# Hybrid decoder layer on one core: attention values with the value matrix as stationary operand, four score banks and a deeper order of steps

## What is computed

```python
proj = jnp.einsum('bsd,de->bse', x, w_in[l])
aq, ak, av, hq, hf, hi_, hg = [proj[..., offsets[j]:offsets[j + 1]] for j in range(len(IN_SIZES))]
a = moba_attention(to_heads(aq), to_heads(ak), to_heads(av), t5_bias)   # softmax(q k / 8 + bias), causal
...
r = hgrn2(...)                                # gated recurrence, RMS norm per head, gate
mix = jnp.einsum('bse,ed->bsd', jnp.concatenate([a, r], axis=-1), w_o[l])
x = layer_norm(DEEPNORM_ALPHA * x + mix, ln1_g[l], ln1_b[l])
moe = hier_moe(x, ...)                        # top-1 group, top-2 of its experts
x = layer_norm(DEEPNORM_ALPHA * x + moe, ln2_g[l], ln2_b[l])
```

## Time and profile before

| | us |
|---|---|
| median of 3 runs (lowest, highest) | 656.98 (656.62, 657.64) |
| the profiled execution, its own time | 655.68 |
| its span | 653.9 |
| PE busy | 616.9 (94%) |
| DVE busy | 475.7 (73%) |
| ACT busy | 377.7 (58%) |
| POOL busy | 110.2 (17%) |
| attention, first scores to first matmul of the output product | 213.4 to 264.4 |

### The profile page before, as it was taken

How to read it: one execution, slowest core, us unless ns; L and a number is a source line. 1 busy time by engine, 2 the same in 40 slices (tenths; PEclk the granted TensorE clock), 3 DMA queues, 4 the chain that set the end, 5 groups by cost and what they waited for, 6 DMA issues and landing times.

```text
span 653.9 us, 9793 instructions
## 1 busy us (share of the span) xinstructions
PE 616.9 (94%) x3747; PEld 497.8 (76%) x3747; DVE 475.7 (73%) x555; ACT 377.7 (58%) x401; POOL 110.2 (17%) x78
## 2 busy tenths in 40 slices
PE   8998999999999999999799997999999999999990
PEld 7877788877767778888577886888888888888860
DVE  3758398884456434446688985889888898888867
ACT  4567333341124666321537785877787777877744
POOL 0012222480000000000077431110111111110000
PEclk9998999999999999999989998999999999999995
DMA  8732123224106000785679999999999999999353
GB/s 329 257 130 76 56 77 117 65 72 71 65 1 191 4 2 1 311 333 193 225 262 419 420 381 364 399 379 391 391 390 392 391 392 402 402 404 364 88 161 128
DMA packets 42413, 155.25 MB, mean 237 GB/s; under 512 B 11923, under 2 KB 12131, under 8 KB 30092
## 3 DMA queue, kind: packets, MB, share of 16 engines
q1 hardware_dynamic: 37500, 138.40, 54.5%
q0 software_dynamic: 4880, 16.39, 9.5%
HBM read 139.96 MB, written 14.81 MB: 237 GB/s over the span
## 4 chain that ended last, share of the span: by engine, by line
PE 78%; DMA 6%; DVE 4%; POOL 4%; ACT 4%; issue 3%; DVEq 0%; SPq 0%; POOLq 0%; ACTq 0%
PE psum L620 21%; PE psum L622 20%; PE psum L621 20%; PE psum L853 3%; PE psum L733 2%; PE psum L1003 2%; DMA misc<-x_dram,slots 2%; DMA acc_dram<-misc,slots 2%; DMA slot_dram<-rec_i,addr_i 1%; PE psum L831 1%; PE psum L763 1%; PE psum L844 1%; PE psum L1020 1%; PE psum L629 1%; POOL slot_dram L553 1%
## 5 line engine op out<-in xcount | busy, mean ns | idle before, releaser
L1669 DVE TENSOR_TENSOR w_lo<-ring,w_hi 128x2048 fp32r<-128x2048 f32 x95 | 216.1, 2289 | 24.0 <-ACT w_hi L1287 23.3
L620 PE MATMUL psum<-w_hi,act_hi 128*128 128x512 f32 x544 | 221.3, 407 | 4.5 <-ACT ring L1199 1.9
L622 PE MATMUL psum<-w_hi,act_lo 128*128 128x512 f32 x544 | 213.2, 392 | 0.0
L621 PE MATMUL psum<-w_lo,act_hi 128*128 128x512 f32 x544 | 213.1, 392 | 0.0
L1287 ACT ACTIVATE w_hi<-ring 128x2048 fp32r<-128x2048 f32 x96 | 182.4, 1916 | 25.2 <-PE psum L622 24.7
L620 PEld LDWEIGHTS psum<-w_hi,act_hi 128*128 128x128 f32 x544 | 102.9, 189 | 32.0 <-issue 4.5
L622 PEld LDWEIGHTS psum<-w_hi,act_lo 128*128 128x128 f32 x544 | 102.5, 189 | 22.2
L621 PEld LDWEIGHTS psum<-w_lo,act_hi 128*128 128x128 f32 x544 | 102.8, 189 | 18.8
L1430 DVE TENSOR_TENSOR w_lo<-ring,w_hi 128x2048 fp32r<-128x2048 f32 x17 | 41.8, 2461 | 33.5 <-ACT w_hi L1136 33.4
L579 POOL DMA_INDIRECT acc_dram<-misc,slots x15 | 24.8, 1654 | 204.2 <-ACT misc L1337 195.4
L1136 ACT ACTIVATE w_hi<-ring 128x2048 fp32r<-128x2048 f32 x17 | 32.5, 1914 | 42.4 <-PE psum L622 40.8
(11 more groups left out here) (235 smaller groups left out, 711.3 us busy)
## 6 DMA issues: line engine op xcount, KB each, us to landing
ring<-in_w_gate SPq DMA_DIRECT2D x32, 1024.0 KB, 11.6
ring<-in_w_up SPq DMA_DIRECT2D x32, 1024.0 KB, 13.5
ring<-in_w_down SPq DMA_DIRECT2D x32, 1024.0 KB, 13.9
ring<-in_w_in SPq DMA_DIRECT2D x13, 1024.0 KB, 6.6
ring<-in_w_o SPq DMA_DIRECT2D x4, 1024.0 KB, 4.8
acc_dram<-ring SPq DMA_DIRECT2D x5, 512.0 KB, 3.6
ring<-in_x SPq DMA_DIRECT2D x2, 1024.0 KB, 6.5
ring<-strip_dram SPq DMA_DIRECT2D x8, 256.0 KB, 4.6
```

Of the source, the lines that this page charges most:

```text
L620: pe.matmul(dst, lh, rh, start=first, stop=False, skip_group_check=True)
L621: pe.matmul(dst, lh, rl, start=False, stop=False, skip_group_check=True)
L622: return pe.matmul(dst, ll, rh, start=False, stop=last, skip_group_check=True)
L1669: dve.tensor_tensor(w_lo[:, v0 % WBUF, :], ring[:, slot, :], w_hi[:, v0 % WBUF, :].bitcast(F32), ALU.subtract).then_inc(s_lo, 1)
```

## The change

**Values** now has the value matrix of a head as the stationary operand (64 columns) and the transposed probabilities as the moving one (128 columns). The output has channels on partitions: the even head of a pair fills partitions 0 to 63, the odd head 64 to 127, in turn matmul by matmul. A pair's result fills one bank, `a % 2`, in the order in which the output product wants it, so the four transposes of the attention result go away.

**The scale.** With queries along the free dimension the division by the row sums can no longer be a broadcast column. Once per pair DVE takes eight reciprocals per partition and copies each 64 times wide (`inverse_sums`, into `prec_wide`), PE multiplies that with the identity into the pair's other bank (`spread_scale`, 8 matmuls), DVE copies the bank to SBUF (`scale_kept`), and then multiplies, splits high and splits low (`mix_scaled`, now three DVE instructions per pair in place of one multiplication per block at the end, with ACT's part of the split moved to DVE). For pairs 0 to 2 this stands among the next pair's steps.

**Four score banks.** Scores alternate between banks 4, 5 and 2, 3 from the third step on, and wait for the DVE of the step before the last.

**The order.** Transposes come two steps behind the scores, values three steps; ACT's copies come two steps behind its exponentials. The `keep_warm` calls at i = 2 are gone, and steps 1, 2 and 3 have ten each. The end of the stage is ordered anew: the last values come between two pieces of the output product.

```diff
+        mix_a = misc[:, 1024:3072].rearrange("p (a s) -> p a s", a=PAIRS)
+        scale_row = misc[:, 3584:4096]
+        prec_wide = misc[:, 3072:3584].rearrange("p (n c) -> p n c", c=DH)
...
+        def score_bank(n):
+
+            step = n // 2
+            return (4 if step == 0 or step % 2 == 1 else 2) + n % 2
...
             def scores(n):
 
                 h, i = unit(n)
-                if n >= 2:
+                if n == 2:
                     pe.wait_ge(s_logit, n)
...
+                elif n >= 6:
+                    pe.wait_ge(s_logit, n - 2)
...
-                if i == 2:
-                    keep_warm(5, 6 + n % 2)
                 pe.wait_ge(s_prob, n + 1)
...
             def values(n):
+
                 h, i = unit(n)
-                pe.wait_ge(s_ptsb, n + 1)
+                a = h // 2
+                pe.wait_ge(s_ptsb, n + 2)
                 if n == 0:
                     pe.wait_ge(s_qklo, 2 * PAIRS)
+                if a >= 1 and i == 0:
+                    pe.wait_ge(s_mixa, 2 * a - 1)
                 for j in range(i + 1):
-                    last = pe.matmul(psum[:, i, h * DH:(h + 1) * DH], pt_buf(h, i)[:, j * P:(j + 1) * P], av[:, j, h * DH:(h + 1) * DH],
-                                     start=(j == 0), stop=(j == i), skip_group_check=True)
-                last.then_inc(s_pv, 1)
+                    for par in range(2):
+                        last = pe.matmul(psum[64 * par:64 * par + 64, a % 2, i * P:(i + 1) * P], av[:, j, (h + par) * DH:(h + par + 1) * DH],
+                                         pt_buf(h + par, i)[:, j * P:(j + 1) * P], start=(j == 0), stop=(j == i), skip_group_check=True)
+                        if j == i:
+                            last.then_inc(s_pv, 1)
+
+            def spread_scale(a):
+
+                pe.wait_ge(s_prec, a + 1)
+                pe.wait_ge(s_mixa, 2 * a)
+                for i in range(T):
+                    for par in range(2):
+                        last = pe.matmul(psum[64 * par:64 * par + 64, (a + 1) % 2, i * P:(i + 1) * P], prec_wide[:, par * T + i, :], ident,
+                                         start=(i == 0), stop=True, skip_group_check=True)
+                last.then_inc(s_scale, 1)
...
-                if 2 <= n < 6:
+                if 2 <= n < 8:
...
-                    keep_warm(10, 2)
+                    keep_warm(10, 0)
                 if n == 10:
                     pe.wait_ge(s_router, 5)
+                if n >= 12 and n % (2 * T) == 4:
+                    spread_scale(n // (2 * T) - 1)
+                if n >= 6:
+                    values(n - 6)
                 for n2 in (n - 4, n - 3):
                     if 0 <= n2 < NU:
-                        values(n2)
-                for n2 in (n - 2, n - 1):
-                    if 0 <= n2 < NU:
                         probs_t(n2)
...
-            pe.wait_ge(s_mixtlo, 2)
+            spread_scale(PAIRS - 1)
+            pe.wait_ge(s_mixtlo, PAIRS + 1)
             for half in range(2):
                 wo_part(0, 2, half)
-            for n in range(4, KD):
-                mix_transpose(n)
-            pe.wait_ge(s_mixtlo, 4)
+            values(NU - 2)
             for half in range(2):
                 wo_part(0, 3, half)
...
+            for n in range(0, NU + 4, 2):
                 if n < NU:
                     probs(n)
                     probs(n + 1)
...
+                if n >= 4:
+                    pt_copy(n - 4)
+                    pt_copy(n - 3)
...
+            def inverse_sums(a):
+
+                cols = slice(2 * T * a, 2 * T * (a + 1))
+                dve.wait_ge(s_prob, 2 * T * (a + 1))
+                dve.wait_ge(s_scale, a)
+                link(dve.reciprocal(prec[:, cols], psums[:, cols]))
+                dve.tensor_copy(prec_wide, prec[:, cols].rearrange("p (n c) -> p n c", c=1).broadcast_to((P, 2 * T, DH))).then_inc(s_prec, 1)
+
+            def scale_kept(a):
+
+                dve.wait_ge(s_scale, a + 1)
+                dve.tensor_copy(scale_row, bank((a + 1) % 2)).then_inc(s_mixa, 1)
+
+            def mix_scaled(a):
+
+                dve.wait_ge(s_pv, 2 * T * (a + 1))
+                dve.wait_ge(s_mixa, 2 * a + 1)
+                dve.tensor_tensor(mix_a[:, a, :], bank(a % 2), scale_row, ALU.mult).then_inc(s_mixa, 1)
+                dve.wait_ge(s_mixa, 2 * a + 2)
+                tiles = lambda ap: ap.rearrange("p (i q) -> p i q", q=P)
+                link(dve.tensor_copy(tiles(act_hi[:, a, :]), turned(mix_a[:, a, :])))
+                dve.tensor_tensor(tiles(act_lo[:, a, :]), turned(mix_a[:, a, :]), tiles(act_hi[:, a, :].bitcast(F32)), ALU.subtract).then_inc(s_mixtlo, 1)
...
+                if n >= 10 and n % (2 * T) == 2:
+                    inverse_sums(n // (2 * T) - 1)
+                if n >= 13 and n % (2 * T) == 5:
+                    scale_kept(n // (2 * T) - 1)
+                if n >= 14 and n % (2 * T) == 6:
+                    mix_scaled(n // (2 * T) - 1)
                 dve.wait_ge(s_score, n + 1)
```

More of the change, by code:

```diff
@@ L830, in scores @@
                         rows = slice(64 * par, 64 * par + 64)
-                        last = pe.matmul(psum[:, 4 + par, ks], q[rows, h // 2, qs], k[rows, h // 2, ks], start=(m == 0), stop=(m == 2),
+                        last = pe.matmul(psum[:, score_bank(n + par), ks], q[rows, h // 2, qs], k[rows, h // 2, ks], start=(m == 0), stop=(m == 2),
                                          skip_group_check=True)
@@ L881, in _ @@
                         pe.wait_ge(s_router, 2)
[L882 to L883 removed]
+                        pe.matmul(psum[:, 1, 0:2 * KD * NL], ones, wg_b.rearrange("p r k n -> p (r k n)"), start=True, stop=True).then_inc(s_wsum, 1)
+                    keep_warm(10, 0)
                 if n == 10:
                     pe.wait_ge(s_router, 5)
+                if n >= 12 and n % (2 * T) == 4:
+                    spread_scale(n // (2 * T) - 1)
+                if n >= 6:
+                    values(n - 6)
                 for n2 in (n - 4, n - 3):
                     if 0 <= n2 < NU:
[L888 to L890 removed]
                         probs_t(n2)
[L893 to L894 removed]
+                if n >= NU:
+                    mix_transpose(n - NU)
+                    mix_transpose(n - NU + 1)
             def y_transpose(i, chunks=range(KD)):
@@ L946, in _ @@
                 for q in range(1, WO_UNITS):
+                    if i == 0 and q == WO_UNITS - 1:
+                        pe.wait_ge(s_mixtlo, KD)
                     for half in range(2):
@@ L1257, in mix_hi @@
             def mix_hi(n):
-                k = (4 + n) % KD
                 act.wait_ge(s_mixt, n + 1)
-                src = bank((4 + n) % 8).rearrange("p (i q) -> p i q", q=P) if k >= 4 else turned(bank((4 + n) % 8))
-                act.activation(act_hi[:, k, :].rearrange("p (i q) -> p i q", q=P), src, ACT.Copy).then_inc(s_mixthi, 1)
-            for n in range(0, NU + 2, 2):
+                act.activation(act_hi[:, 4 + n, :], bank(mix_bank(n)), ACT.Copy).then_inc(s_mixthi, 1)
+            for n in range(0, NU + 4, 2):
                 if n < NU:
@@ L1267, in _ @@
                     probs(n + 1)
-                if n == NU:
-                    mix_hi(0)
-                    mix_hi(1)
-                if n >= 2:
-                    pt_copy(n - 2)
-                    pt_copy(n - 1)
-            mix_hi(2)
-            mix_hi(3)
+                if n >= 4:
+                    pt_copy(n - 4)
+                    pt_copy(n - 3)
+                if n >= NU:
+                    mix_hi(n - NU)
+                    mix_hi(n - NU + 1)
             hi(16)
-            for n in range(4, KD):
-                mix_hi(n)
             hi(17)
@@ L1618, in centred_router @@
                 for r in range(2):
-                    part = psum[:, 3, r * KD * NL:(r + 1) * KD * NL].rearrange("p (k n) -> p n k", k=KD)
+                    part = psum[:, 1, r * KD * NL:(r + 1) * KD * NL].rearrange("p (k n) -> p n k", k=KD)
                     dve.tensor_reduce(w_sum[:, r], part, AX.X, ALU.add).then_inc(s_router, 1)
```

57 lines of the change are left out of this document (19 added, 38 removed).

## The result

The changed kernel takes **659.79 us** (median of 20 runs, 655.95 to 663.89) against 656.40 us of the kernel before (20 runs beside them, 653.23 to 659.19): a ratio of 1.0054, 95% interval 1.0037 to 1.0072. The profiled execution took 663.89 us, the longest of the 20, with a span of 662.0 us and a mean granted clock of 0.968 (0.981 before).

The account below looks back on a forecast made before the run. PE, busy 94% of the span, was taken as the bound, with removed work returning as waits for ACT's copies. -1.7 us at full clock plus 2.8 for clock falls gave +1.1: median 656.98 to 658.1 us, range 653.8 to 661.5.

Parts of the forecast that it names:

- PE's work: In attention, PE loses 9.3 us of work through cheaper values, fewer dummies and no result transposes, less the added `spread_scale`.
- the rival of 0.117: Values: the array's halves don't run side by side, so each product costs 0.117 us; 667.1 us in all, chance 0.06.
- DVE's burst: Scale, product and split add 3.2 us per pair on DVE, making its scores of i = 3 about 1 us late.
- The waits: PE waits for ACT's copies at values behind i = 0 (2.3 us), plus smaller waits, 3.1 a pair; 2.8 in the drain.
- The stepping: Engine queues stepped through attention's 16 steps by trace durations: output product starts at 264.1 instead of 264.4 us.
- -1.7: Change in us at full clock, through the output product's first unit, ending at 276.0 instead of 277.2, corrected by 0.5.
- two and a half falls: Attention's new waits drop the clock to 1.2 GHz two and a half times at 1.1 us each: +2.8 us.
- 1.35 us are let pass and 1.86 are not: PE idle of 1.35 us at 215.30 brought no lower clock; idle of 1.86 us at 57.70 was followed by one.
- The clock holds: Rival: attention stays at full clock despite the new waits, giving -1.7 us, 655.3 us; chance 0.23.
- The bursts hide: Rival: DVE's extra work fits its idle time and ACT's order doesn't bind, giving 647.7 us; chance 0.08.
- The clock falls everywhere: Rival: clock falls also around 0.6 us waits and at attention's start, five times 1.1 us, 660.8 us; chance 0.08.
- The rule on copies: By the skill's rule, DVE's wide copy and high part would be some 0.2 us shorter each, forecast about 657.5 us.

Follow-up runs that it names:

- e1: Changed kernel with ACT's two copies of transposed probabilities ahead of its two exponentials in each step: 646.65 us, ratio 0.9859 to the kernel before.
- e2: Changed kernel with twelve dummy matmuls between the scores of i = 0 and the values behind them, four times: 654.70 us, ratio 0.9982.
- e7: e1 with all values products of one half of the array ahead of the other's, instead of in turn: 650.96 us, ratio 0.9906.
- e6: e1 with two score banks in place of four: 652.69 us, ratio 0.9922 to the kernel before.
- e9: Changed kernel with two score banks in place of four, ACT's order as it is: 659.87 us, ratio 1.0051.
- e4: Kernel before without its eight times five dummy matmuls at i = 2: 653.78 us, ratio 0.9956.
- e3: Changed kernel without DVE's product, high part and low part for the first three pairs: 655.79 us, ratio 0.9993.
- e5: Kernel before with ACT's copies ahead of its exponentials, distances between steps unchanged: 655.37 us, ratio 0.9982.
- e8: e1 with 20 of its 30 dummy matmuls at the start of attention left out: 648.65 us, ratio 0.9876.
- e10: e1 without DVE's product, high part and low part for the first three pairs: 650.20 us, ratio 0.9887.

## Why the prediction was right in its place and short in its size

**PE's work: the prices right, the sum too high.** Values cost 0.051 to 0.057 us from start to start (0.058 predicted; the rival of 0.117 is out), `spread_scale` (1.09 - 0.28) / 15 = 0.054. The sum was too high all the same: without the transposes (1.8 us), which lay behind the stage, and with the last values (1.0) moved out of it, the terms give 9.3 - 1.8 + 1.0 = 8.5 us less in the stage, and e1 shows 48.70 - 41.91 = 6.8. That e1's median gain is 9.3 us too is chance. No single term is to blame. Added up from start to start in the timelines, waits left out, PE's work in the stage is 49.0 us before and 42.1 in e1, 6.9 less, and against the prediction's terms the values miss 0.4 us, scores and recurrence transposes (put down as unchanged) 0.3 each, the dummies 0.2, the transposes of probabilities 0.2, `spread_scale` 0.1. The prediction charged 0.09 us for leaving the form of the values, and nothing for the operations ahead of it: eight recurrence transposes with values behind them take 1.04 us to the next start, and took 0.87.

**DVE's burst: right.** From the scores of i = 2 on, the kept scale begins at 231.50 - 229.64 = 1.86 us (1.90 predicted), i = 3's first head at 4.74 (4.96).

**The waits: right in place, a little too long.** 1.91 us in place of 2.3, 0.21 in place of 0.56, 2.39 in place of 2.8; the third one, 0.3 us for i = 2, does not come in the third and fourth pair. At the higher clock the second pair took 9.93 us (10.0 predicted), and the third, in e2, 11.50 (11.7).

**The stage at full clock.** The stepping had 264.1 - 213.4 = 50.7 us. The profiled execution of the changed kernel did not keep the clock. e2, which did, has 51.94 with 48 dummies, of which the first twelve cost 1.1 us: without them 50.8, as stepped. But the old kernel, stepped the same way, came out 0.5 us late, so the stage was to be 0.8 us shorter than before, and it is 0.2. The first unit behind the stage, from its first matmul to ACT's next split of weights, takes 283.07 - 270.55 = 12.52 us (12.5 in e1 and e2 too) against 277.50 - 264.47 = 13.03 before: 0.5 us gained where I had 0.9 (12.8 to 11.9). So -1.7 was rather -0.2 - 0.5 = -0.7.

**The clock: the mis-sized term.** I had two and a half falls at 1.1 us, +2.8. The profiled execution has four in the stage where before had none, and one more behind it. What one costs can be read in four ways. Among the 20 runs of the changed kernel the time rises by 0.70 us for each 0.001 of mean clock less (655.95 us at 0.976, 661.67 to 663.89 at 0.968), and one stretch of 3.41 us at half speed is 0.5 x 3.41 / 660 = 0.0026 of the mean clock: 1.8 us. In the stage, 56.83 - 50.8 = 6.0 us for four: 1.5 each. e7's at the start of attention took 1.6. And in work ahead of the stage that no run changed, 4 of the 12 profiled executions have a stretch at 59 us (before, changed, e6, e9): their attention starts at 213.5 us in the mean, that of the others at 211.9, 1.6 later. My 1.1 had assumed that the doubled work is thin and eats waits; the windows show PE busy 3.41 of 3.41, 6.43 of 6.82 and 3.42 of 3.42 us there, so nearly half of each is lost, 1.7 us. The number was short as well: the median clock of the 20 runs is 0.9725 against 0.9805 in 58 runs of before, 0.008 / 0.0026 = 3.1 more falls. -0.7 + 3.1 x 1.5 = +4.0 us, near the measured 3.5. Only the rival in which the clock falls everywhere had priced that a fall can follow the wait at the start of attention (1.35 us, at 215.62 as at 215.30 before): it did in the changed kernel, e4, e7 and e9, not in the profiled executions of the others. And in e3 a stretch at 0.50 begins at 233.51 us, 0.7 us behind the end of a wait of 1.17. So the prediction's reading that 1.35 us are let pass and 1.86 are not does not hold: the length of a wait alone does not decide it.

**The rivals.** "The clock holds" is what e2 forces: 654.70 us against 655.3, with dummies that cost 1.1 us of it and a gain of 0.7 in place of 1.7, so the closeness is partly luck. "The bursts hide" is what e1 makes true by ACT's order: 646.65 against 647.7; the prediction had named that order as what speaks against it, and here too the closeness is luck, since less work went than the 9.3 us. "The clock falls everywhere", 660.8 us at 1.1 each, came nearest to the median with fewer falls at a higher price.

**The rule on copies.** The Trainium skill (VectorE: DVE Perf Modes, "Mode 2×_2P — use both read ports for one tensor") would have a float32 operation with one source, within SBUF, pass its values at twice the rate of one with two sources. The trace agrees, once the fixed part of an instruction is taken off. The wide copy and the high part took 0.43 us, two sources 0.69; the kept scale, a copy too but out of PSUM, also took 0.69. By instruction and shape (count, busy us, mean ns), the changed kernel has for 512 values

```profile
L1665 DVE TENSOR_TENSOR act_lo<-misc,act_hi 128x512 fp32r<-128x512 f32 x4 | 2.8, 692 | 0.1
L1664 DVE CAST act_hi<-misc 128x512 fp32r<-128x512 f32 x4 | 1.7, 427 | 0.1
```

and the kernel before for 128 values

```profile
L1785 DVE TENSOR_TENSOR misc<-misc 128x128 f32<-128x128 f32 x1 | 0.3, 291 | 0.0
L1753 DVE CAST act_lo<-cst 128x128 fp32r<-128x128 f32 x1 | 0.2, 219 | 0.0
```

so 384 values more cost 427 - 219 = 208 ns with one source and 692 - 291 = 401 with two. The prediction took 0.5 and 0.6 us for the wide copy and the high part from L1870 and 0.6 for the kept scale: 0.07 and 0.17 too long, and 0.09 too short.

## What to carry to other kernels

An engine's queue is a promise in order: ask of every operation that stands behind another whether it needs that one. Here copies whose input had been ready stood behind exponentials that wait for the newest scores, and that tied PE's oldest work to its newest. The added banks brought nothing until this order was changed (e9 against the changed kernel, e6 against e1), and the order brought little in the old kernel (e5); what the added distance gives by itself was not measured. Count what a new wait does to the clock at 1.5 to 1.8 us for each fall where PE is otherwise full, look at the mean clock of all runs and not only of the profiled one, and try to remove the wait (e1, -13 us) before filling it with dummies (e2, -5 us).

## What the runs showed of the hardware

- Products of 64 stationary and 128 moving columns that alternate between the halves of the array start in pairs, 0.007 us apart in a group of 16 and 0.035 in one of 12, a pair every 0.109 us. With one half's products all ahead of the other's, a group of 16 takes 1.53 us in place of 1.04; starts 0.05 to 0.06 us apart in its middle suggest that the second half begins during the last ones of the first.
- Stretches at the lower clock came some 50 to 140 us behind the edited stage where e1 had fewer (e8 from 387.1 us, e10 from 316.7 us on), in work that was not changed. A saving of 2.2 us in a stage (e8) did not show in the median of 5 runs.
- The wait at the start of attention, 1.35 us long in each kernel, was followed by a stretch at 1.2 GHz in the profiled executions of the changed kernel, e4, e7 and e9 and in none of the other eight; e1 and e7 have the same program up to there.
- A stretch of 3.41 us at 1.2 GHz cost 1.5 to 1.8 us where PE was full.
